# Stick-breaking and block attention of a decoder step: running sum in the accumulator, rounded triangle products, heads in turn

## What is computed

```python
def stick_breaking_attend(q, k_all, v_all, q_start):
    ...
        z = jnp.einsum('bqhd,bkhd->bhqk', qb, kb) * scale
        ...
        strict = jnp.arange(kend)[None, :] < tpos[:, None]
        log_beta = jnp.where(strict, jax.nn.log_sigmoid(z), NEG)
        log_keep = jnp.where(strict, jax.nn.log_sigmoid(-z), 0.0)
        later = lax.cumsum(log_keep, axis=3, reverse=True) - log_keep
        w = jnp.exp(log_beta + later)
        outs.append(jnp.einsum('bhqk,bkhd->bqhd', w, vb))
```

## Time and profile before

| | us |
|---|---|
| median of three runs | 2083.14 |
| lowest and highest run | 2082.85, 2085.31 |
| the profiled execution | 2081.41 |
| its span, from the first to the last instruction | 2079.6 |
| PE busy in the span | 1910.9 (92%) |
| DVE busy | 1131.5 (54%) |
| ACT busy | 716.8 (34%) |
| MoBA stage, about | 245 to 391 of the span |
| stick-breaking stage, about | 1304 to 1484 of the span |

### The profile page before, as it was taken

How to read it: one execution, slowest core, us unless ns; L and a number is a source line. 1 busy time by engine, 2 the same in 40 slices (tenths; PEclk the granted TensorE clock), 3 DMA queues, 4 the chain that set the end, 5 groups by cost and what they waited for, 6 DMA issues and landing times.

```text
span 2079.6 us, 34107 instructions
## 1 busy us (share of the span) xinstructions
PE 1910.9 (92%) x13244; PEld 1660.2 (80%) x13244; DVE 1131.5 (54%) x2433; ACT 716.8 (34%) x1300; POOL 13.6 (1%) x27
## 2 busy tenths in 40 slices
PE   6999889899999979999999898787799999979997
PEld 5587555798999979988489896343598999979987
DVE  7982154547777762253322395555557777762254
ACT  3211233454333342253322222444454333342252
POOL 0000000000000000000000000000000000000000
PEclk9999878899999999999999957799999999999998
DMA  4122557412222222131122310655212222222121
GB/s 165 60 46 87 181 189 274 158 46 71 89 84 81 68 97 83 55 112 66 42 90 82 106 52 11 238 197 208 79 51 72 84 87 82 68 96 84 56 81 46
DMA packets 77852, 204.13 MB, mean 98 GB/s; under 512 B 12530, under 2 KB 14754, under 8 KB 77218
## 3 DMA queue, kind: packets, MB, share of 16 engines
q1 hardware_dynamic: 75442, 189.70, 27.3%
q0 software_dynamic: 2288, 12.72, 1.7%
HBM read 190.81 MB, written 10.40 MB: 97 GB/s over the span
## 4 chain that ended last, share of the span: by engine, by line
PE 83%; DVE 12%; ACT 3%; issue 2%; DMA 1%; DVEq 0%; POOL 0%; ACTq 0%; POOLq 0%
PE psum L395 39%; PE psum L559 12%; PE psum L1485 6%; PE psum L403 5%; PE psum L2028 3%; PE psum L1229 2%; PE psum L790 2%; PE psum L1205 1%; PE psum L481 1%; PE psum L1322 1%; PE psum L1299 1%; PE psum L2169 1%; DVE sb_arena_r L355 1%; PE psum L495 1%; PE psum L1060 1%
## 5 line engine op out<-in xcount | busy, mean ns | idle before, releaser
L395 PE MATMUL psum<-sb_a_sb_r,sb_ring_r 128*128 128x288 f32 x1280 | 259.1, 295 | 0.0
L395 PE MATMUL psum<-sb_a_sb_r,sb_arena_r 128*128 128x288 f32 x1280 | 257.0, 296 | 0.0
L395 PE MATMUL psum<-sb_y_sb_r,sb_arena_r 128*128 128x288 f32 x704 | 207.2, 294 | 11.0 <-DVE sb_arena_r L355 10.9
L395 PE MATMUL psum<-sb_y_sb_r,sb_ring_r 128*128 128x288 f32 x704 | 208.6, 296 | 0.0
L395 PEld LDWEIGHTS psum<-sb_a_sb_r,sb_ring_r 128*128 128x128 f32 x1280 | 206.5, 188 | 0.0
L395 PEld LDWEIGHTS psum<-sb_a_sb_r,sb_arena_r 128*128 128x128 f32 x1280 | 204.2, 188 | 0.0
L355 DVE TENSOR_TENSOR sb_ring_r<-sb_ring,sb_ring_r 128x1024 fp32r<-128x1024 f32 (+1 forms) x78 | 101.6, 1306 | 159.7 <-ACT sb_ring_r L352 158.9
L352 ACT ACTIVATE sb_ring_r<-sb_ring 128x1024 fp32r<-128x1024 f32 (+1 forms) x78 | 87.4, 1124 | 286.4 <-PE psum L395 221.3
L559 PE MATMUL psum<-sb_arena_r 128*128 128x288 f32 x960 | 160.8, 302 | 8.3 <-DVE sb_arena_r L355 8.3
L395 PE MATMUL psum<-sb_arena_r,sb_ring_r 128*128 128x288 f32 x1056 | 145.4, 299 | 20.9 <-DVE sb_arena_r L355 20.9
L395 PEld LDWEIGHTS psum<-sb_arena_r,sb_ring_r 128*128 128x128 f32 x1056 | 143.6, 193 | 21.3 <-issue 21.3
(11 more groups left out here) (418 smaller groups left out, 3412.6 us busy)
## 6 DMA issues: line engine op xcount, KB each, us to landing
sb_ring<-w SPq DMA_DIRECT2D x166, 512.0 KB, 3.6
sb_ring<-wd SPq DMA_DIRECT2D x32, 704.0 KB, 4.1
sb_arena<-moba_v SPq DMA_DIRECT2D x64, 256.0 KB, 4.8
sb_arena<-sb_v SPq DMA_DIRECT2D x64, 256.0 KB, 5.3
sb_ring<-moba_k SPq DMA_DIRECT2D x32, 256.0 KB, 4.0
sb_a_sb<-moba_k SPq DMA_DIRECT2D x32, 256.0 KB, 5.4
sb_ring<-sb_k SPq DMA_DIRECT2D x32, 256.0 KB, 4.0
sb_a_sb<-sb_k SPq DMA_DIRECT2D x32, 256.0 KB, 5.2
```

The lines of the kernel that those rows point to most:

```text
L395: ins = e.eng.matmul(out[:, half, :], fr(w[p][:, k, :]), fr(x[q][:, k, cols]), start=(first and k == 0 and i == 0), stop=(last and k == kb ...
```

## The change

In both stages the heads of a pair now alternate unit by unit (g = 0, 1), so two units of equal width follow each other, and the output products of the two are issued together after the second, in odd iterations. Head g writes partitions 64g to 64g+63 of the accumulator.

```diff
-        UNITS = [(hh, i) for hh in range(NH) for i in range(4)]
+        UNITS = [(2 * c + g, i) for c in range(NH // 2) for i in range(4) for g in range(2)]
...
-                if u >= 2:
-                    hh, i = UNITS[u - 2]
+                if u >= 3 and u % 2 == 1:
+                    hh, i = UNITS[u - 3]
...
                     for j in range(i + 1):
-                        last = pe.matmul(psum[r0:r0 + 64, 4, i * P:(i + 1) * P],
-                                         vt[:, j, hh * HD:(hh + 1) * HD], ptb[u % 2][:, j, :],
-                                         start=(j == 0), stop=(j == i))
+                        for g in range(2):
+                            last = pe.matmul(psum[64 * g:64 * g + 64, 4, i * P:(i + 1) * P],
+                                             vt[:, j, (hh + g) * HD:(hh + g + 1) * HD], ptb[(u - 3 + g) % 4][:, j, :],
+                                             start=(j == 0), stop=(j == i))
```

```diff
+                if u >= 3 and SBU[u - 3][1]:
+                    j = SBU[u - 3][1]
+                    pe.wait_ge(d_ready, u - 2)
+                    for z in (s_hi, s_lo):
+                        pe.matmul(psum[:, 2 + (u - 3) % 2, j * P:TP], fr(rest_r), fr(z[(u - 3) % 3][:, 0:TP - P * j]),
+                                  start=False, stop=True, skip_group_check=True)
...
-                    last = pe.matmul(psum[:, 2 + b, 0:P], tri, s_t[b][:, 0:P], start=True, stop=True)
-                    if j < 3:
-                        pe.matmul(psum[:, 2 + b, P:n], tri, s_t[b][:, P:n], start=True, stop=False)
-                        last = pe.matmul(psum[:, 2 + b, P:n], ones, r_t[b][:, P:n], start=False, stop=True)
+                    pe.wait_ge(lo_ready, u)
+                    for i, z in enumerate((s_hi, s_lo)):
+                        last = pe.matmul(psum[:, 2 + (u - 1) % 2, j * P:TP], fr(tri_r), fr(z[(u - 1) % 3][:, 0:TP - P * j]),
+                                         start=(j == 3 and i == 0), stop=True, skip_group_check=True)
...
-                    if u >= 4:
-                        act.wait_ge(ow_ready, u - 3)
                     act.activation(w_t[b][:, 0:n], w_t[b][:, 0:n], ACT.Exp).then_inc(w_ready, 1)
+                if 1 <= u <= len(SBU):
+                    n = TP - P * SBU[u - 1][1]
+                    act.wait_ge(sp_ready, u)
+                    if u >= 2:
+                        act.wait_ge(tt_ready, u - 1)
+                    act.activation(fr(s_hi[(u - 1) % 3][:, 0:n]), s_t[:, 0:n], ACT.Copy).then_inc(hi_ready, 1)
...
                     if u >= 4:
-                        v.wait_ge(ow_ready, u - 3)
+                        v.wait_ge(ow_ready, (u - 4) // 2 + 1)
...
-                    if j:
-
-                        r = r_t[1 - b]
-                        do(v.tensor_copy(r[:, P:2 * P], s_t[b][:, 0:P]))
-                        if j < 3:
-                            do(tt(r[:, 2 * P:n + P], s_t[b][:, P:n], r_t[b][:, P:n], ALU.add))
                 between(samples, u, len(SBU) + 1, DUE_C["dve"])
+                if 1 <= u <= len(SBU):
+                    v.wait_ge(hi_ready, u)
+                    dve_low(e, s_t[:, 0:n], s_hi[at][:, 0:n], s_lo[at][:, 0:n], lo_ready)
```

More of the change, by code:

```diff
@@ L1280, in build @@
         pb = [cut(unit_at + i * 512, 512) for i in range(2)]
-        ptb = [cut(unit_at + (2 + i) * 512, 512).rearrange("p (j n) -> p j n", j=4) for i in range(2)]
+        ptb = [cut(unit_at + (2 + i) * 512, 512).rearrange("p (j n) -> p j n", j=4) for i in range(4)]
         stat = small[:, 8:64]
@@ L2387, in dve_hgrn @@
                 do(tt(out, out, gh[:, hs, :], ALU.mult))
-        e_t, s_t, r_t = ([cut(unit_at + (2 * j + i) * 512, 512) for i in range(2)] for j in range(3))
-        z_t = [cut(unit_at + 3072 + i * 512, 512) for i in range(3)]
-        w_t = [cut(unit_at + 4608, 512), rstd[:, 0:512]]
-        assert unit_at + 4608 + 512 <= 26300
-        DUE_C = {"pe": (8, (1, 2, 8, 9, 9, 10)), "act": (8, (3, 4, 7, 8)), "dve": (8, (3, 5, 6, 7, 10, 11))}
-        zs_ready, zc_ready, nz_ready, l_ready, sp_ready, tt_ready, d_ready, w_ready, ow_ready, ocp_ready = (
+        e_t, s_hi, s_lo, z_t = ([cut(unit_at + (3 * j + i) * 512, 512) for i in range(3)] for j in range(4))
+        s_t = cut(unit_at + 6144, 512)
+        w_t = [e_t[2], rstd[:, 0:512]]
+        tri_r, rest_r = (cut(unit_at + 6656 + i * P, P) for i in range(2))
+        assert unit_at + 6656 + 2 * P <= 27400
+        DUE_C = {"pe": (8, (1, 2, 8, 9, 9, 10)), "act": (8, (3, 4, 7)), "turned": (8, (9,)), "dve": (8, (3, 5, 6, 7, 10, 11))}
+        zs_ready, zc_ready, nz_ready, l_ready, sp_ready, tt_ready, d_ready, w_ready, ow_ready, ocp_ready, hi_ready, lo_ready, tri_ready = (
             sem(x) for x in ("zs_ready", "zc_ready", "nz_ready", "l_ready", "sp_ready", "tt_ready", "d_ready", "w_ready",
-                             "ow_ready", "ocp_ready"))
-        SBU = [(hh, j) for hh in range(NH) for j in (3, 2, 1, 0)]
+                             "ow_ready", "ocp_ready", "hi_ready", "lo_ready", "tri_ready"))
+        SBU = [(2 * c + g, j) for c in range(NH // 2) for j in (3, 2, 1, 0) for g in range(2)]
         def pe_sb_prompt(e):
@@ L2424, in pe_sb_prompt @@
+                if 1 <= u <= len(SBU):
+                    j = SBU[u - 1][1]
+                    if u == 1:
+                        pe.wait_ge(tri_ready, 1)
+                    if u >= 3 and j == 3:
                         pe.wait_ge(d_ready, u - 2)
-                    last = pe.matmul(psum[:, 2 + b, 0:P], tri, s_t[b][:, 0:P], start=True, stop=True)
-                    if j < 3:
-                        pe.matmul(psum[:, 2 + b, P:n], tri, s_t[b][:, P:n], start=True, stop=False)
-                        last = pe.matmul(psum[:, 2 + b, P:n], ones, r_t[b][:, P:n], start=False, stop=True)
+                    pe.wait_ge(lo_ready, u)
+                    for i, z in enumerate((s_hi, s_lo)):
+                        last = pe.matmul(psum[:, 2 + (u - 1) % 2, j * P:TP], fr(tri_r), fr(z[(u - 1) % 3][:, 0:TP - P * j]),
+                                         start=(j == 3 and i == 0), stop=True, skip_group_check=True)
@@ L2430, in pe_sb_prompt @@
                     last.then_inc(tt_ready, 1)
-                if u >= 2:
-                    hh, j = SBU[u - 2]
-                    r0, c, n = 64 * (hh % 2), hh // 2, TP - P * j
+                if u >= 3 and u % 2 == 1:
+                    hh, j = SBU[u - 3]
+                    c, n = hh // 2, TP - P * j
                     pe.wait_ge(w_ready, u - 1)
-                    if hh % 2 == 0 and j == 3 and c >= 1:
+                    if j == 3 and c >= 1:
                         pe.wait_ge(ocp_ready, c)
-                    pe.matmul(psum[r0:r0 + 64, 4, j * P:TP], vt[:, j, hh * HD:(hh + 1) * HD], w_t[u % 2][:, 0:n],
-                              start=(j == 3), stop=True, skip_group_check=True).then_inc(ow_ready, 1)
+                    for g in range(2):
+                        last = pe.matmul(psum[64 * g:64 * g + 64, 4, j * P:TP], vt[:, j, (hh + g) * HD:(hh + g + 1) * HD],
+                                         w_t[g][:, 0:n], start=(j == 3), stop=True, skip_group_check=True)
+                    last.then_inc(ow_ready, 1)
@@ L2445, in copy_out @@
             def copy_out(c):
-                act.wait_ge(ow_ready, 8 * (c + 1))
+                act.wait_ge(ow_ready, 4 * (c + 1))
                 act.activation(y[:, 4 + c, 0:TP], psum[:, 4, :], ACT.Copy).then_inc(ocp_ready, 1)
@@ L2461, in act_sb_prompt @@
                     act.activation(e_t[b][:, 0:n], e_t[b][:, 0:n], ACT.Ln, bias=one_col).then_inc(l_ready, 1)
+                between(samples, u, len(SBU) + 1, DUE_C["turned"])
                 if u >= 2:
```

34 lines of the change are left out of this document (13 added, 21 removed).

## The result

The changed kernel takes 2095.09 us, the median of five runs (2090.93 to 2095.67), against 2083.14 before (that median is of five runs too, 2082.85 to 2085.31). The ratio is 1.0051, with a 95% interval of 1.0037 to 1.0066. It is slower by half a per cent where 8 us less were forecast.

A forecast was written before the change was run, and what follows sets the result against it. It took MoBA as mostly bound by PE and stick-breaking by no engine, three waiting for each other in turn. MoBA -7, A +3, B -4.6 and the rest +0.7 gave -8 us on 2083.1, so 2075; range 2060 to 2092.

The forecast's parts named there:

- MoBA, -7: MoBA stage: paired outputs overlap fully and halve their PE time, 7 us less in sum; bounds -3 and -18.
- rival 3: The two array halves wait for each other, MoBA's gain falls by 10, A's pair wait doubles: 2092; chance 0.05.
- The three B: MoBA, L1229 to L1410: narrower scores, one transpose less and paired outputs save 1.3 us, three times, -3.9.
- The four A: MoBA, L1410 to L1229: paired outputs save, four more transposes cost; -0.5 us each, four times, -2.0.
- The start: Start of the MoBA stage: narrower first units, scores of 256 in place of 384 and 512, -1.2 us.
- B, -4.6: Stick-breaking, L1229 to L1212: three stretches of 10.4 us against 35.8 together; bounds -7 and -2.
- A, +3: Stick-breaking, L1212 to L1229: four stretches of 31.9 us against 124.4 together; bounds -6 and +12.
- The clock: Stick-breaking A: 29.7 us at full clock, 34.1 at half; the middle, 31.9, taken because the clock comes back.
- The new wait: Stick-breaking A: DVE's subtraction of even units waits for the output pair, late twice; +0.5 us, +1.8 more at half clock.
- The rest, +0.7: Stick-breaking's ends: small DVE operations +0.5, narrower first units -0.5, last L1229 at half clock +0.7; other stages nothing.
- its own sign: Any stage other than MoBA and stick-breaking moving by more than 2 us would make the sum's frame wrong.
- Rival 1: Stick-breaking A stays at half clock up to L1229: A 34.1 us, sum +7, kernel 2090; chance 0.22.

The follow-up runs named there:

- both kernels without the wait: The changed kernel with four `w_t` buffers in place of two, ratio 1.0001, and the changed kernel with the output pair issued ahead of the triangle product, ratio 0.9986.
- after: The changed kernel itself, with both the MoBA and the stick-breaking edits, against the kernel before: 2095.09 us, ratio 1.0051.
- MoBA filled: The changed kernel with the output pair ahead of the triangle product, plus two filling products in each of three iterations of eight in MoBA: 2077.72 us, ratio 0.9966.
- the one with four buffers: The changed kernel with four `w_t` buffers in place of two, so DVE's subtraction needs the pair before the last one: 2084.22 us, ratio 1.0001.
- the MoBA part alone: The kernel before with only the MoBA edits, stick-breaking as before: 2081.72 us, ratio 0.9983.
- Output first: The changed kernel with the stick-breaking output pair issued ahead of the triangle product: 2081.89 us, ratio 0.9986.
- Output first with filling: The changed kernel with the output pair ahead of the triangle product, plus a 512-column filling product in five of eight stick-breaking iterations: 2078.19 us, ratio 0.9973.

## Why the prediction was wrong, step by step

**MoBA, -7: it gave -5.0.** The mechanism and the direction were right: full overlap of two 64-wide products, and rival 3 falls. To compare term by term I cut at L1212 in both kernels. The three B gave -3.2 (38.7 to 35.5) for -3.9.

The four A gave -2.1 (84.6 to 82.5) for -2.0, and that agreement is luck. The prediction counted 10 output blocks against 5 pairs and four transposes more in an A, -0.4. The traces have 15 blocks against 12 side by side (30 records of L1322, 24 of L1323) and one transpose more (17 and 18), which by the same prices is -2.1 in each A. So PE lost five times the work that was counted, and about three quarters of it did not shorten A.

The start gave +0.4 for -1.2, the term that was mis-sized. The narrower first units did save their 1.2 us, but the second L1205 ran at half clock, where before it had run at full clock (chain in order of time, before and after):

```profile
259.02 1.85 PE psum L1205 x16
```

```profile
257.68 3.57 PE psum L1205 x16
```

**B, -4.6: it gave -4.6.** 10.09, 11.12 and 9.99 around the 10.4 that was worked out from PE's list and DVE's.

**A, +3: it gave +16.** This is the step that failed, in two of its terms.

- *The clock.* I had 29.7 at full and 34.1 at half clock and took the middle, on the argument that at half clock the same products fill twice the time, which is when the clock came back before. The rows say otherwise: 0.54 to 0.62 over whole stretches, although PE is busy in 26.2 of 35.6 us. Its busy share was the same before (23.88 of 32.6 us in the second A) at a granted clock of 0.84, so the busy share of a stretch did not tell which of the two clocks it would have. The reading of the earlier trace rows was also loose: the scan ends at 1375.82, so they hold its last 0.8 us only, and PE's pause there is its wait for s (L2499) until 1377.7. From the middle to half: 2.2 us an A.
- *The new wait.* I had +0.5, and +1.8 more at half clock, together 2.3, from two late pairs. There are three in a period, 14.2 / 4 = 3.6 us of idle DVE, and without the wait A is 3.2 shorter. That is 0.9 more than the term. The sum of the other terms stands: 34.1 less 2.3 is 31.8, and both kernels without the wait measured 31.9. That doesn't make each of them right. DVE's idle time for ACT's high part, for one, is 4.1 us in each of the first three A and 1.2 in the fourth, in after, where the high parts without cover were put at 1.2 in each; other terms must have been too high, and which is not shown.

The two come to 3.1 us an A, 12.4 in the four, of the 13 that A is off. Of the 22 us between the forecast of -8 and the +14.1 of the profile, A makes 13, the rest 7 and MoBA 2.

**The rest, +0.7: it gave +7.8.** Start +2.5, tail +1.0, dense stage +2.8, between the stages +1.4. The prediction put nothing at the dense stage and between the stages, and by its own sign (a stage other than the two that moves by more than 2 us) the dense stage breaks the frame of its sum. The other kernels show what each goes with.

- *Between the stages, +1.4.* It belongs to the MoBA part. From MoBA's last L1229 to the last DMA ahead of stick-breaking it takes 920.6 to 920.9 us in the three kernels without that part, and 922.3 or more in the ten with it and without filling in MoBA. The dense stage behind MoBA starts at a granted clock of 0.57 in place of 0.72, and with MoBA filled, at 0.72 again and 921.1 us. So the MoBA part is worth 3.6 and not 5.0 in the profile, close to the 3.5 by the ratio of its own run.
- *Start of stick-breaking, +2.5.* 1.1 stand ahead of PE's first triangle product: the two small operations on DVE and the first high and low part. 1.4 stand behind it, where the second L1205 takes 3.38 us in place of 1.85. Eight of the nine kernels with rounded parts have 14.6 to 14.7 us here; the one with four buffers has 12.4 and a second L1205 of 1.85, with the same program up to there. So the second part can fall either way.
- *Dense stage, +2.8.* It goes with the clock at its start, but not with a stick-breaking stage near half clock. The kernel with the MoBA part alone, at 0.79 to 0.94 in its A, starts it at 0.58 and takes 595.2 us for it, where after takes 595.4 (before 592.7):

```profile
1486.10:1492.10 6.00, 6.00 (x28) 6.00 (x29) 6.00 (x11) 6.00 (x14) 0.00 (x0) 0.58 0.52 155
```

All thirteen other kernels take 594.3 to 595.7, and the one profile of before is alone with its 592.7. Before was profiled once, in an execution 1.7 us under its median, so how much of the 2.8 is due to the change stays open.

**The rivals.** Rival 1 held by its own test, A over 34 with a low clock up to L1229. It gave 2090, 5 us short, since it too had the small wait term and an end of +1.5. Its weight of 0.22 was too low, and its point, that it decides from about three quarters of A at half clock, was met with room. Before the run, the Trainium skill, "TensorE: Matmul & The Clock Gate", section "HAM oscillation - how this bites in real kernels", stood beside it: each burst behind a pause starts cold, again and again. The trace agrees in kind with its numbers of 0.54, 0.57, 0.58 and 0.62 in the four A. What no sentence of mine had asked is what the cold burst stands in front of. Output first shows that a clock of 0.58 costs much less where the burst isn't waited for: 0.8 us an A against the same kernel with filling, in place of 2.6.

**What stays open.** What sets the clock in B (0.85 to 0.95) and not in A was not tried apart. Nor was the tail, and what makes the dense stage start at 0.54 to 0.66 in every kernel but the one before.

## What to carry to other kernels

Side by side products halve PE's time only where PE is what is waited for. In a stage where three engines wait for each other, first look at what the pair is put in front of: here issuing it ahead of a product that had to wait anyway was worth 13 us, more than MoBA and B had gained together (9.6, less the 1.4 behind MoBA). When a change takes work from PE but not its pauses, price every product on the chain at half clock, and those at the stage's two ends too: at the start of both stages thinner units left the second L1205 at half clock, and behind MoBA the dense stage paid 1.4 us. And when two suspected causes are at hand, run all four combinations: each remedy alone took away most of what A had lost (2.6 and 3.2 of 4.0 us), and together they did not take more than all of it.

## What the runs showed of the hardware

- Added work can shorten a stretch: a 512-column product in five iterations of eight raised the granted clock from 0.57 to 0.84 in the second A and took 2.6 us off the mean of 35.1, and cost 1.8 us a stretch where the clock was already 0.79 to 0.94.
- Two plain fp32 products of 64 output channels each, in the two halves of the array, start at the same time (1385.26) and are shown with the same end. Per record of 128 columns that is 0.064 us in place of 0.128.
- A stage can leave a lower clock to the next one: behind MoBA with paired outputs the dense stage's first six microseconds stand at 0.57 in place of 0.72, and the way to the next stage takes 1.4 us longer; filling products inside MoBA gave 0.72 and 1.2 of the 1.4 back.
- Near the start of the program there is more spread than in the stages: in the kernels with the changed MoBA code the first L1212 starts between 256.2 and 262.7 us, though all are the same program up to there save for MoBA's filling products. Output first with filling is the one at 256.2, and its profiled execution of 2070.64 lies 7.5 us under its median of 2078.19. Stretches, from start to start inside a stage, can be compared; two single times of whole programs can't.
